# A recurrent mixing layer: gate projections and latents moved ahead of z, and the group ends interleaved

## What is computed

```python
def token_mix(h, ...):
    qkv, z, b_raw, a_raw, q_lat, kv_lat, k_pe, gate_a, gate_b = jnp.split(h @ w_in, offsets, axis=-1)
    y_a = gated_deltanet(qkv, z, b_raw, a_raw, ...) @ w_branch_a
    y_b = mla(q_lat, kv_lat, k_pe, ...) @ w_branch_b
    ...
def gated_deltanet(...):      # 8 heads of 128, in chunks
    q, k, v = split(silu(causal_dwconv(qkv, conv_w)));  q, k = l2_norm(q), l2_norm(k)
    beta = sigmoid(b_raw);  g = -exp(a_log) * softplus(a_raw + dt_bias)
    o = gated_delta_rule(q, k, v, g, beta)
    return rms_norm(o, out_gain) * silu(z)
def mla(...):
    q = rms_norm(q_lat, q_lat_gain) @ w_q_up          # latent width 384
    kv = rms_norm(kv_lat, kv_lat_gain) @ w_kv_up      # latent width 256
    ...
```

## Time and profile before

| | before |
|---|---|
| median of three runs | 3191.54 us |
| the profiled execution | 3193.39 us, with a span of 3191.6 us from first to last instruction |
| mean granted TensorE clock | 0.956 of full |
| busy: TensorE products, VectorE, ScalarE, GpSimd | 93%, 73%, 43%, 11% |
| DMA | 628 MB read, 197 GB/s over the span |

### The profile page before, as it was taken

How to read it: one execution, slowest core, us unless ns; L and a number is a source line. 1 busy time by engine, 2 the same in 40 slices (tenths; PEclk the granted TensorE clock), 3 DMA queues, 4 the chain that set the end, 5 groups by cost and what they waited for, 6 DMA issues and landing times.

```text
span 3191.6 us, 62155 instructions
## 1 busy us (share of the span) xinstructions
PE 2981.5 (93%) x24632; PEld 2812.8 (88%) x24632; DVE 2325.2 (73%) x3887; ACT 1377.9 (43%) x2145; POOL 341.5 (11%) x378
## 2 busy tenths in 40 slices
PE   5999888999999998789999999699989999999898
PEld 5999775999999997669999999599956899999798
DVE  7998554558977775555788888588977578777654
ACT  3446322544444552243444446444654444444342
POOL 0021001010100210100102011002023100202001
PEclk9999887999999998899999999899999999999899
DMA  9995201348967650015687885288501378776353
GB/s 341 349 342 185 75 2 66 126 165 321 342 234 281 213 172 28 23 61 188 233 311 274 306 322 170 73 314 312 174 6 34 132 257 319 255 263 237 97 187 133
DMA packets 172712, 631.95 MB, mean 198 GB/s; under 512 B 19168, under 2 KB 19552, under 8 KB 172000
## 3 DMA queue, kind: packets, MB, share of 16 engines
q1 hardware_dynamic: 123696, 450.75, 40.1%
q10 hardware_dynamic: 48816, 178.41, 16.1%
HBM read 628.04 MB, written 1.05 MB: 197 GB/s over the span
## 4 chain that ended last, share of the span: by engine, by line
PE 82%; DVE 13%; ACT 2%; issue 1%; DMA 1%; DVEq 0%; POOL 0%; ACTq 0%
PE psum L555 22%; PE psum L557 21%; PE psum L556 21%; DVE w_lo L523 3%; DVE xl L1943 2%; PE psum L2098 2%; PE psum L573 1%; PE psum L2085 1%; DVE ada_w L602 1%; PE psum L574 1%; DVE qkv L1049 1%; PE psum L2100 1%; PE psum L1290 1%; DVE bc L1943 1%; PE psum L579 1%
## 5 line engine op out<-in xcount | busy, mean ns | idle before, releaser
L555 PE MATMUL psum<-h_hi,w_hi 128*128 128x256 f32 x4464 | 1251.1, 280 | 7.6 <-DVE h_lo L1835 4.6
L557 PE MATMUL psum<-h_lo,w_hi 128*128 128x256 f32 x4464 | 1247.3, 279 | 0.0
L556 PE MATMUL psum<-h_hi,w_lo 128*128 128x256 f32 x4464 | 1247.0, 279 | 0.0
L523 DVE TENSOR_TENSOR w_lo<-raw,w_hi 128x1024 fp32r<-128x1024 f32 x852 | 1059.5, 1249 | 156.8 <-ACT w_hi L510 156.4
L510 ACT ACTIVATE w_hi<-raw 128x1024 fp32r<-128x1024 f32 x852 | 873.5, 1054 | 393.9 <-DMA raw<-stream_dram 240.6
L555 PEld LDWEIGHTS psum<-h_hi,w_hi 128*128 128x128 f32 x4464 | 839.7, 188 | 18.2 <-issue 8.7
L556 PEld LDWEIGHTS psum<-h_hi,w_lo 128*128 128x128 f32 x4464 | 840.0, 188 | 0.0
L557 PEld LDWEIGHTS psum<-h_lo,w_hi 128*128 128x128 f32 x4464 | 839.8, 188 | 0.0
L557 PE MATMUL psum<-u_lo,w_hi 128*128 128x256 f32 x1584 | 442.4, 279 | 0.0
L555 PE MATMUL psum<-u_hi,w_hi 128*128 128x256 f32 x1584 | 442.3, 279 | 0.0
L556 PE MATMUL psum<-u_hi,w_lo 128*128 128x256 f32 x1584 | 441.9, 279 | 0.0
(11 more groups left out here) (365 smaller groups left out, 3541.5 us busy)
## 6 DMA issues: line engine op xcount, KB each, us to landing
raw<-stream_dram SPq DMA_DIRECT2D x852, 512.0 KB, 4.3
ada_w<-ada_dram ACTq DMA_DIRECT2D x328, 512.0 KB, 4.7
tmp<-c_dram ACTq DMA_DIRECT2D x8, 512.0 KB, 3.5
x<-x_dram SPq DMA_DIRECT2D x1, 1024.0 KB, 10.8
ctx_x<-ctx_dram ACTq DMA_DIRECT2D x1, 1024.0 KB, 4.7
means<-means_dram ACTq DMA_DIRECT2D x1, 1024.0 KB, 4.7
out_dram<-tmp SPq DMA_DIRECT2D x1, 1024.0 KB, 3.9
const<-const_dram SPq DMA_DIRECT2D x1, 720.5 KB, 13.7
```

What stands on the lines that cost most here:

```text
L523: p.nc.vector.tensor_tensor(p.w_lo[:, slot].rearrange("p k m -> p (k m)"), p.raw[:, slot], p.w_hi[:, slot].rearrange("p k m -> p (k m)").b ...
L555: mm(out, p.w_hi[:, slot, k], hi, start=start, stop=False, skip_group_check=skip)
L556: mm(out, p.w_lo[:, slot, k], hi, start=False, stop=False, skip_group_check=skip)
L557: return mm(out, p.w_hi[:, slot, k], lo, start=False, stop=stop, skip_group_check=skip)
```

## The change

It does the following, in both layers of the first block:

- The weight units of project are reordered: q, k, v, then the seven latent tiles (b and a among them), then z. The sums of squares come after unit 23, and their root at t = 26. Sixteen length rows go out two at a time after the units 28 to 35, over three banks. ScalarE's gate activations run at t = 31 ahead of the eight silu of z, VectorE's gate steps at t = 33, and the column products after unit 36. The rope angles of layer 0 move to t = 27.
- In gdn the tokens go from VectorE to ScalarE, the product of q with exp to GpSimd. Group 2's row tiles are put ahead of group 1's states. Group 2's pairs wait for one output at a time. The first and second values and the outputs use other tiles and banks for that.
- GpSimd squares the latents after group 2's transposes; TensorE sums them in 16 rows ahead of group 2's states, one inverse and one root serve both latents, and two rows are spread ahead of group 2's outputs. Scaling and splitting of the latents lie beside group 2's outputs.
- The output norm (sums, inverse, root, eight spread rows, scaling) moves into up, between the q products.

```diff
-    proj = np.concatenate([qkv, z, q_lat, kv_lat, k_pe, k_pe, ba], 1)
+    proj = np.concatenate([qkv, q_lat, kv_lat, k_pe, k_pe, ba, z], 1)
...
 def project_tensor(p, pe, st):
-    with pe.Fori(1, 4) as g:
+    with pe.Fori(1, 3) as g:
...
+    for t in range(24, 39):
+        one(t // 8, t % 8)
+        for h in range(2 * (t - FIRST_LENGTH), 2 * (t - FIRST_LENGTH) + 2) if 0 <= t - FIRST_LENGTH < 8 else ():
+            length_row(p, pe, st, h)
+        if t == GATE_COLS:
+            gate_cols(p, pe, st)
+
+FIRST_LENGTH = 28
+GATE_COLS = 36
+LENGTH_BANKS = (2, 3, 6)
...
 def length_row(p, pe, st, t):
-    if t >= 4:
-        pe.wait_ge(p.sem["normed"], st.at("normed") + t - 3)
+    if t >= 3:
+        pe.wait_ge(p.sem["normed"], st.at("normed") + t - 2)
...
 def project_scalar(p, act, st):
+        if t == 31:
+            gate_scalar(p, act, st)
         act.wait_ge(p.sem["unit_done"], u0 + t + 1)
-        out, func = (p.z[:, t - 24], ACT.Silu) if t < 32 else (p.lat[:, t - 32], ACT.Copy)
+        out, func = (p.lat[:, t - 24], ACT.Copy) if t < 31 else (p.z[:, t - 31], ACT.Silu)
...
 def project_vector(p, dve, st):
+        if t == 33:
+            gate_vector(p, dve, st)
+        for h in range(2 * (t - FIRST_LENGTH - 1), 2 * (t - FIRST_LENGTH)) if 0 < t - FIRST_LENGTH <= 8 else ():
...
 def gdn_scalar(p, act, st):
+    def tokens(gq):
+        act.wait_ge(p.sem["cols_ready"], a("cols_ready") + 1)
+        for i in range(GROUP):
+            h = gq * GROUP + i
+            act.wait_ge(p.sem["turned_done"], a("turned_done") + h + 1)
+            act.wait_ge(p.sem["decay_ready"], a("decay_ready") + h + 1)
+            k0, k1, v0, v1 = (p.psum[:, i, n * P : n * P + P] for n in range(4))
+            f(p.v_beta[:, i, 0:P], v0, ACT.Copy, scale=p.cols[:, 0, 0, h : h + 1])
...
+    decays(0, 0, GROUP)
+    tokens(0)
+    first(0)
+    corners(0)
+    first_values(0)
+    decays(1, 0, 2)
+    states(0)
+    decays(1, 2, GROUP)
+    outs(0)
+    tokens(1)
+    first(1)
...
+    corners(1)
+    first_values(1)
+    states(1)
+    act.wait_ge(p.sem["lat_var"], a("lat_var") + 2)
+    f(p.var[0:16], p.var[0:16], ACT.Sqrt).then_inc(p.sem["lat_root"], 1)
+    squares(0)
+    latents(0, LAT_Q)
+    outs(1)
+    squares(1)
+    latents(LAT_Q, LAT_Q + LAT_KV)
...
 def gdn_tensor(p, pe, st):
+    row_tiles(0)
+    pair_tiles(0)
+    inverse(0)
+    row_tiles(1)
+    states(0)
+    outs(0)
+    pair_tiles(1)
+    inverse(1)
+    for t in range(LAT_Q + LAT_KV):
+        pe.wait_ge(p.sem["lat_sq"], a("lat_sq") + t + 1)
+        ins = mm(p.psum[0:16, 0, 0:T], p.pick("row", t // LAT_Q), p.lat_sq[:, t], start=t == 0, stop=t == LAT_Q + LAT_KV - 1)
+    ins.then_inc(p.sem["lat_sum"], 1)
+    states(1)
+    pe.wait_ge(p.sem["lat_root"], a("lat_root") + 1)
+    for b in range(2):
+        mm(p.psum[:, 1 + 2 * b, 0:T], ident[0:16, b : b + 1].to_broadcast([16, P]), p.var[0:16], start=True,
+           stop=True).then_inc(p.sem["lat_rows"], 1)
+    outs(1)
...
 def gdn_vector(p, dve, st):
+    levels(0)
+    decays(1)
+    values(0)
+    scores(1)
+    levels(1)
+    lat_inverse(p, dve, st)
+    values(1)
+    lat_split(p, dve, st, 0, LAT_Q)
+    for h in range(GROUP):
+        o_gate(p, dve, st, h)
+    lat_split(p, dve, st, LAT_Q, LAT_Q + LAT_KV)
...
 def up_tensor(p, pe, st):
+        if u == 0:
+            o_sums(p, pe, st.gdn)
         if u:
             total(2 * u - 2)
             total(2 * u - 1)
+        for h in range(2 * (u - 2), 2 * (u - 1)) if u >= 2 else ():
+            o_length(p, pe, st.gdn, h)
...
 def up_vector(p, dve, st):
+    for h in range(GROUP, HEADS):
+        o_gate(p, dve, st.gdn, h)
     for s in range(6):
         split_lo(p, dve, u0 + AHEAD + s)
+        if s == 0:
+            o_inverse(p, dve, st.gdn)
+        for h in range(2 * (s - 2), 2 * (s - 1)) if s >= 2 else ():
+            o_scale(p, dve, st.gdn, h)
```

More of the change, by code:

```diff
@@ L110, in constants @@
     put("q_scale", np.where(i < HEADS, 1.0 / P, 1.0)[:, None])
+    put("lat_scale", np.where(i == 0, 1.0 / (LAT_Q * P), 1.0 / (LAT_KV * P))[:, None])
     put("eps", EPS)
@@ new lines, in lat_split @@
+def lat_split(p, dve, st, first, last):
+    a, v, gain, b = st.at, p.nc.vector, st.par(p, "lat_gain"), first // LAT_Q
+    dve.wait_ge(p.sem["lat_rows"], a("lat_rows") + b + 1)
+    for t in range(first, last):
+        v.scalar_tensor_tensor(
+            p.lat[:, t], p.lat[:, t], gain[:, t : t + 1], p.psum[:, 1 + 2 * b, 0:T], ALU.mult, ALU.mult
+        ).then_inc(p.sem["lat_scaled"], 1)
+    for t in range(first, last):
+        dve.wait_ge(p.sem["lat_rounded"], a("lat_rounded") + t + 1)
+        v.tensor_tensor(p.lat_lo[:, t], p.lat[:, t], p.lat_hi[:, t].bitcast(F32), ALU.subtract).then_inc(
+            p.sem["lat_ready"], 1)
@@ new lines, in latents @@
+    def latents(first, last):
+        for t in range(first, last):
+            act.wait_ge(p.sem["lat_scaled"], a("lat_scaled") + t + 1)
+            f(p.lat_hi[:, t], p.lat[:, t], ACT.Copy).then_inc(p.sem["lat_rounded"], 1)
+    act.wait_ge(p.sem["cols_ready"], a("cols_ready"))
+    f(p.exp_cols[:], p.cols[:, 1, 1], ACT.Exp).then_inc(p.sem["exp_cum"], 1)
+    decays(0, 0, GROUP)
[6 more added lines that the diff above has]
+    decays(1, 2, GROUP)
@@ L1281, in gdn_tensor, with row_tiles @@
-    for gq in range(HEADS // GROUP):
-        at = lambda name, per: a(name) + gq * per
-        if gq:
-            pe.wait_ge(p.sem["out_ready"], a("out_ready") + gq * GROUP)
+    ident, rows = p.c("ident"), p.rows[0 : 32 + HEADS]
+    halves = low, high = [slice(0, HALF), slice(HALF, P)]
+    def row_tiles(gq):
         for i in range(GROUP):
@@ L1307, in gdn_tensor, with inverse @@
             ins.then_inc(p.sem["turned_done"], 1)
-        halves = [slice(0, HALF), slice(HALF, P)]
+    def inverse(gq):
+        at = lambda name, per: a(name) + gq * per
         for i in range(GROUP):
@@ L1344, in gdn_tensor @@
         merged = LEVELS * PAIRS
-        low, high = halves
         for i in range(GROUP):
@@ L1392, in gdn_tensor, with o_length @@
[L1392 to L1396 removed]
+def o_length(p, pe, gdn, h):
+    if h == 0:
+        pe.wait_ge(p.sem["o_root"], gdn.at("o_root") + 1)
+    if h >= 2:
+        pe.wait_ge(p.sem["oa_ready"], gdn.at("oa_ready") + h - 1)
+    p.nc.tensor.matmul(
+        p.psum[:, 4 + h % 2, 0:T], p.c("ident")[0:16, h : h + 1].to_broadcast([16, P]), p.rinv[0:16], start=True, stop=True
+    ).then_inc(p.sem["len_row"], 1)
```

348 lines of the change are left out of this document (175 added, 173 removed).

## The result

| | before | after |
|---|---|---|
| median of the runs | 3189.32 us (4 runs, 3186.16 to 3197.84) | 3142.51 us (4 runs, 3139.53 to 3148.56) |
| profiled execution: time, span, clock | 3193.39, 3191.6 us, 0.956 | 3144.26, 3142.5 us, 0.966 |

The ratio is 0.9854, 95% interval 0.9839 to 0.9868: 46.8 us or 1.5% faster. The forecast was 3124 us, in a range of 3108 to 3142. The sign and seven tenths of the gain are there (49.1 us in the profiled executions where the steps gave 67.9), and the median lies just outside the range. 18.8 us are missing.

What follows compares the result with a forecast made beforehand. TensorE, 82% of the chain, was taken as the bound, through its waits and low clock. Steps summed to -35.5 [-32.4], together -67.9 us, from 3193.4 to 3125.5; the median lies 1.9 lower, so 3124 us, range 3108 to 3142.

Steps and rivals of the forecast that it cites:

- A: Project, layer 1 [layer 0]: head of gdn -8.8, length rows +2.8, columns +1.2, stalls +2.0; sum -2.8 [+0.8] us.
- B: Group 1 up to level 0: rows and pairs 10.7 us, tokens on ScalarE, level 0 at 15.1; -4.6 [-5.1] us.
- C: From group 1's last w and u to group 2's levels: 24.0 us becomes 17.5 in layer 1; -6.5 [-5.9] us.
- Levels: Levels of both groups, taken at full level, 20.5 us each with their end: -4.8 [-5.8] us.
- The rival that kept them as they were: The four first levels of the groups stay at today's half level: 10.6 us in all, within a rival of chance 0.12.
- D: From group 2's w and u to the end of the q products: 53.1 us becomes 36.3 in layer 1; -16.8 [-16.4] us.
- the second: More half level: group 2's row tiles drag states and outputs (+6.8), first levels stay as today (+10.6): 3141 us; chance 0.12.
- The first: Full level through group 1's row tiles: rows and pairs 7.6 us instead of 10.7, 3.1 more gained per layer, 3118; chance 0.15.

Runs made afterwards that it cites:

- the kernel with two edits: Changed kernel plus 22 constant products in TensorE's wait ahead of the attention, and VectorE's length multiplies ahead of its low split: 3129.7 us, 0.9796.
- the last fill: Changed kernel with three edits, plus 3 constant products behind the attention's first two length rows and one in each of its first four heads: 3134.4 us, 0.9814.

## Why the prediction was right and where it failed

**A** held in its waits: I worked out 1.7 us for row 9 in layer 1, and the row above shows 1.60; in all 6.4 us of wait stand for the 7.6 of both layers. The term that failed is the level. In layer 1 there are some 4 us at half level before and 3.4 after. Before they lay in the head of gdn, 9.30 us at 0.79 with TensorE busy for 3.83; now they lie on the weight stream, where TensorE is always busy. Without waits and half level the stage takes 61.05 us (the kernel with two edits), so of 64.41 - 61.05 = 3.4 us 1.6 are the wait and 1.8 the level. The forecast less its own stalls was 60.5: rows and columns were 0.5 short.

**B** came out 0.6 better through two errors. "I take its 10.7 us for them": rows and pairs took 8.9, from 1194.18 to 1203.10. And "with a scale from a tile, which no row has at this size, I take 0.2": the tokens follow each other at 0.25. And the stage took 12.9 to 16.1 us in other executions, with the level, so that 14.49 came so near to 15.1 is in part luck.

```profile
424.58 0.37 ACT L1317 ACTIVATE v_beta<-psum,cols 128x128 f32<-128x128 f32 x1 [3.68 <-PE psum L1420]
424.85 0.36 ACT L1318 ACTIVATE v_beta<-psum,cols 128x128 f32<-128x128 f32 x1
425.10 0.37 ACT L1319 ACTIVATE k_tok<-psum,beta_exp 128x128 f32<-128x128 f32 x1
```

The copies without a tile's scale start 0.18 apart, so the operand costs 0.07. The Trainium skill (ScalarE: Activation LUTs, What ACT_TABLE_LOAD costs) puts each such pointer operand at 93 ns. The length of one copy agrees, 0.37 us with it and 0.28 without; the distance between copies grew less. An estimate of the distance by that figure is 0.27, which makes C 18.6, where the trace has 18.2.

**Levels** is the step that failed by arithmetic. "Levels and end are 3.3 + 17.2 = 20.5": the 17.2 were counted from 1245.64, the start of the second pair of level 1; its first pair starts 0.94 us sooner, at 1244.68, and a group at 1.00 takes 21.33 us. Four times 0.83 (21.33 less 20.5) are 3.3 of the 6.6. The other 3.3 are "I give both groups the full level": three first levels of four still fell, after a wait of 1.7 us, for some 3 us each. The rival that kept them as they were (10.6 us) was wrong too.

**C** is right to 0.7 us. Of its 5.8 us in layer 1 TensorE's busy time is 3.4 (19.31 to 15.88) and its idle time 2.3 (4.69 to 2.36). The forecast didn't tell the two apart: it summed work at full level and so took the 3.4 us of level for granted. The rows' new place covers no wait, as the run with the rows put back shows (the same 2.4 to 2.6 us of idle time), so the 2.3 must come from the rest of the change, of which no run tried a part alone.

**D** is right to 0.3 us of 36.6, with no wait on sums, root or rows but one of 0.31 us on ScalarE's root of the latents. Of the 16.5 us 10.4 are waits that are gone (10.7 us of idle time before, 0.3 after) and 6.1 are busy time (21.00 + 21.40 us to 36.31): there were 20.5 us at half level before, 16.4 of them under work, and none after.

**The attention** is what the prediction left out. Its last paragraph looked for a saved stretch that comes back as a wait in the tail of up; that tail is the same to 0.1 us. What came back is half level in the stage behind it, 9.7 us, and this alone is half of what is missing. The forecast's sum had no term for it, which is a term of nothing without a reason; it is the step that failed most. None of the rivals had it: the second asked for half level in states, outputs and first levels, and the states and outputs ran at 1.00. The first, full level through group 1's row tiles, holds in some executions (12.86 us) and not in others; its chance of 0.15 was the wrong form for what varies from run to run.

Taken together: of the 49.1 us gained 33.0 are TensorE's idle time, so the waits that the change took away are two thirds of the gain, as the forecast's argument has it. The other 16.1 are busy time. There were 65 us less at half level, but 17 of them lay in waits and gave nothing; the 47 under work, at the 0.48 us from above, are worth some 23 (an estimate). That leaves some 7 us of busy time added, in project and in the q products, where the rows now go out two at a time. Level is thus at most half of the gain, and it would be 9.7 us more without what the attention lost. The forecast saw the clock in rows 2 and carried it stage by stage, but only through stages that the change touches.

What stays open is why the level comes back after 10 or 14 us in one place and 24 in another with TensorE busy alike, and so whether the attention can be kept at full level for certain.

## What to carry to other kernels

Before you credit a stage with removed waits, write down TensorE's busy and idle time in it, and its us at half level, 2(1 - clock) times its length, before and after. Only half level under work costs time: in step C more of the gain was level than waits, in step D it was the other way round, and the length of the stages alone shows neither. Cut the windows also behind the last stage that you change, since a stage of light products can lose in level what was won ahead of it. And read a repeated step's start from its first piece, with the piece before it in sight: a landmark one pair late, times four, was over 3 us here.

## What the runs showed of the hardware

The Trainium skill (TensorE: Matmul & The Clock Gate, The HAM clock gate) says that activity releases the low level. Here TensorE was busy 13.36 of 13.60 us at 1.2 GHz, and 19.87 of 23.88, with the attention's products, and the level did not come back before the end of these stretches; the measurement decides. What in these products makes the difference no run tried. With 3.5, 7.9, 11.6, 13.8 and 20.1 us of half level the same stage took 28.8, 30.3, 32.1, 32.9 and 35.9 us, and 28.1 with none, there with the products of the last fill added.

Useless work can win back more than it takes in the stage behind it: with 1.8 us of constant products in each layer, outside any wait, the attentions took 30.4 and 30.3 us in place of 36.1 and 35.9. The whole, at 0.9835, shows neither the cost nor the gain.
